# A mixture-of-experts decoder block in split float32: low and high rows side by side in the twelve full groups of experts

## The chip, the cores and the metric

The kernel runs on one NeuronCore of one Trainium2 chip. The time of a run is the device time in microseconds (us) of that core. The kernel before took 3754.32 us as the median of three runs (3741.82 to 3757.93). Beside these runs stands one profiled execution, from which every duration below is read.

## The reference, cut to what matters

The reference is a two-part decoder: a first block (attention, a linear recurrence, and a layer of 16384 experts), then a second block (a state-space mixer and sparse attention). The change concerns the layer of experts alone. Each of 256 tokens picks 128 experts out of 16384, 16 for each of 8 heads:

```python
    def expert_block(args):
        hx, ex, wx = args
        ug = jnp.take(u, ex, axis=0)
        act = jax.nn.gelu(jnp.einsum('thkd,td->thk', ug, hx)) * wx
        vg = jnp.take(vt, ex, axis=0)
        return jnp.einsum('thk,thkd->td', act, vg)
```

## The kernel before, in words

**All experts, densely.** The kernel does not gather experts. It multiplies all tokens with all 128 tiles of 128 experts (`peer_u`, 2048 inputs each), takes the gelu, multiplies with a dense matrix of weights that is zero where a token did not pick an expert, and multiplies the result with `peer_v`. Tiles 0 to 31 are treated earlier, under other work. Tiles 32 to 127 are the **full groups**: 12 passes of one loop, each with 8 tiles of `peer_u` (chunks 0 to 7) and then the 8 chunks of `peer_v` that belong to them (chunks 8 to 15).

**Split numbers.** In this stage a float32 number is written as high + low, both of the type float32r. A product of w and F is then three matmuls: w_hi times F_hi, w_hi times F_lo, w_lo times F_hi. The rows F (2048 inputs by 256 tokens, as 16 blocks of 128 by 256) are split once into `Fhi` and `Flo`. The weights are split as they arrive: a chunk lands by DMA in one of the four slots of `ring`, ScalarE (ACT) copies half a chunk (8 blocks of 128 by 128) to `vhi` (`v_high`, L1182), and VectorE (DVE) subtracts, `vlo` = chunk - `vhi` (`v_low`, L1732). `vhi` and `vlo` have two halves each, so a half is filled again only when TensorE (PE) has used it: `v_used` counts the halves that PE has finished, `vhi_ready` and `vlo_ready` the halves that are filled.

**A tile of experts on PE** (`gemm_experts`, L498): per half a wait for `vhi_ready`, 16 matmuls of 256 columns with `vhi` (against `Fhi` and `Flo` in turn, L509 and L510), a wait for `vlo_ready`, 8 matmuls of 256 columns with `vlo` (L514). All 48 add up in the first 256 columns of one PSUM bank. Banks are used in turn (tile n in bank n mod 4).

**A chunk of `peer_v` on PE** (`gemm_rows`, L540): per half 8 matmuls of 512 columns with `vhi` (L557, L558) and 4 with `vlo` (L564). They need the hidden values of the group as `Ghi` and `Glo`, and `g_ready` counts the tiles for which both stand.

**What ACT and DVE do beside it.** In the loop over the 8 tiles, ACT has for tile n: `half_high(n+1, 0)`, `half_high(n+1, 1)`, `gelu(n)` (from the bank into `GL`, L1222, then a drain), `gelu_high(n-1)` (`GL` to `Ghi`, L1227). DVE has: `half_low(n+1, 0)`, `vector` (half of a product with a vector for a modulation that is needed later, L1809), `half_low(n+1, 1)`, `weigh(n)` (`GL` times the dense weights, L1792), `gelu_low(n-1)` (`GL` - `Ghi` into `Glo`, L1797, then a drain). In both lists an instruction that waits holds up everything behind it on its engine: each engine takes its instructions in the written order. There is no planner; the order is that of the code. `GL` has two places, tile n in place n mod 2, and `gelu_free` keeps ACT from filling a place again too early.

**The DMA queue** is SP's (L450 to L457): it loads chunk c + 4 into a slot when PE has freed it, and after every second chunk the next megabyte for `vector`, once DVE has freed that buffer (`vec_free`).

Of the kernel before, what the change touches and what calls it, by code (L numbers as in the profile page):

```python
# [19 lines left out]
F32 = mybir.dt.float32  # L20
F32R = mybir.dt.float32r
# [3 lines left out]
ALU = mybir.AluOpType  # L25
ACT = mybir.ActivationFunctionType
AX = mybir.AxisListType.X

P = 128
T = 256  # L30
D = 2048
KT = D // P
# [79 lines left out]
def build(nc, a):  # L112

    ctx = ExitStack()
    with ctx:
        def sb(name, shape, dt=F32):
            return ctx.enter_context(nc.sbuf_tensor(name, shape, dt))
# [4 lines left out]

        ring = sb("ring", [P, R, KT, P])
        x = sb("x", [P, KT, T])
        rows = ExitStack()
        with rows:
            H = rows.enter_context(nc.sbuf_tensor("H", [P, KT, T], F32))
        Flo = sb("Flo", [P, KT, T], F32R)
        scale_row = H[0:1, 0:8, :].rearrange("p a (b c) -> p (a b) c", b=2)
        beside = ExitStack()  # L130
        with beside:
            head_vec = beside.enter_context(nc.sbuf_tensor("head_vec", [P, 3, D], F32))
# [36 lines left out]
        var = sb("var", [P, 2, T])  # L169
        sd = sb("sd", [P, 2, T])  # L170
        rstd = sb("rstd", [P, 2, T])
        NA = 18800
        BELOW = 2 * T + 2 * (8 * T + 4 * 512)
        shared = ExitStack()
        with shared:
            arena = shared.enter_context(nc.sbuf_tensor("arena", [P, NA], F32))
        below = sb("below", [P, BELOW])
        Ghi2 = sb("Ghi2", [P, 8, T], F32R)
        Glo2 = sb("Glo2", [P, 8, T], F32R)
        Fhi = sb("Fhi", [P, KT, T], F32R)  # L180
        above = sb("above", [P, NA - BELOW - 32 * T])
        banks = [ctx.enter_context(nc.psum_tensor(f"bank{i}", [P, 512], F32)) for i in range(4)]
        WA = ctx.enter_context(nc.psum_tensor("work_a", [P, 512], F32))
# [27 lines left out]
        r = Region()  # L211
# [22 lines left out]
        r = Region()  # L234
# [3 lines left out]
        GL = rstd  # L238
        spread_at = r.at
        spread = r(2, P, 64)  # L240
        r = Region(spread_at)
        hid = r(2, 8, T)
        Wg = r(2, 4, 8, 64)
        vbuf = hid.rearrange("p a b c -> p a (b c)")
        assert r.at == BELOW
        G_hi, G_lo = [Ghi, Ghi2], [Glo, Glo2]
        r = Region(5 * T)
        k12 = r(2, HEADS, P)
# [14 lines left out]
        r = Region()  # L263
# [18 lines left out]
        r = Region()  # L282
# [8 lines left out]
        r = Region(ssm_at - 2 * PAIRS * 16)  # L291
# [4 lines left out]
        r = Region()  # L296
# [11 lines left out]
        r = Region(nsa_at)  # L308
# [15 lines left out]
        bank_free = [sem(f"bank{i}_free") for i in range(4)]  # L324
# [13 lines left out]
        def s(name):  # L338

            if name not in S:  # L340
                S[name] = sem(name)
            return S[name]

        for name in ("consts_ready cond_ready prod_ready biased merged_scaled "
                     "disc_e disc_saved c_col_ready scale_in_psum scale_row scale_col lam_ready cond_loaded disc_loaded w1b_used "
                     "squares_ready scaled_squares sums_ready var_ready sd_ready scaled_ready f_in_psum f_ready "
                     "log1p_ready gatew_loaded qk_ready vt_ready cm_ready scores_ready negmax_ready "
                     "exps_ready probs_ready xc_ready gates_in_psum lru_u_ready lru_t_ready lru_sq_ready "
                     "ly_ready lru_done vrows_in_psum vrows_ready pt_in_psum pt_ready attn_in_psum attn_ready "
                     "k_loaded peerq_ready s_in_psum s_ready vs_ready vs_exp picked_ready cols_in_psum hot_ready "  # L350
                     "fhi_ready flo_ready hot_used spread_copied block_copied early_gelu gelu_ready weighed ghi_ready g_ready vhi_ready vlo_ready v_used y_done y_turned y_clear sz_made hhi_ready h_ready whi_ready wlo_ready half_done ssm_loaded disc_a disc_b disc_c disc_done "
                     "masks_built u_ready bu_in_psum bu_read frac_ready table_ready z_ready q_ready "
                     "y_pair gelu_free glu_free y_read y_gelu sig_ready w1_loaded kv_ready vr_in_psum vr_ready "
                     "b1e_ready cmp_gelu cmp2_in_psum kc_ready vc_in_psum gt_in_psum vg_ready q_ready2 "
                     "sn_in_psum negmax2 exps2 probs2 ptn_in_psum ptn_ready on_in_psum sz_ready combined "
                     "out_ready stored").split():
            s(name)
# [3 lines left out]
        def meet(eng, state):  # L361
# [7 lines left out]
                       dve=('lru_done', 's_ready', 'g_ready', 'combined'))  # L369
# [111 lines left out]
        def _(pe):  # L481
            mm = nc.tensor.matmul
# [14 lines left out]

            def gemm_experts(i, n, before):  # L498

                out = banks[n % 4][:, 0:T]  # L500
                pe.wait_ge(bank_free[n % 4], uses[n % 4] + before + n // 4 + 1)
                for half in range(2):
                    q = 64 + 32 * i + 2 * n + half
                    u_hi, u_lo = [w[:, half].rearrange("p k n -> p (k n)").rearrange("p (k n) -> p k n", k=8)
                                  for w in (vhi, vlo)]
                    pe.wait_ge(s("vhi_ready"), q + 1)
                    for k in range(8):
                        kk = 8 * half + k
                        mm(out, u_hi[:, k, :], Fhi[:, kk, :], start=(kk == 0), stop=False)  # L509
                        mm(out, u_hi[:, k, :], Flo[:, kk, :], start=False, stop=False)  # L510
                    pe.wait_ge(s("vlo_ready"), q + 1)
                    for k in range(8):
                        kk = 8 * half + k
                        last = mm(out, u_lo[:, k, :], Fhi[:, kk, :], start=False, stop=(kk == KT - 1))  # L514
                        if half == 1 and k == 0:
                            last.then_inc(slot_free[n % R], 1)
                    last.then_inc(s("v_used"), 1)

            def gemm_split(stage, i, pos, c, out, bank, need=None, halves=(0, 1), rows=None):

# [91 lines left out]
            for kt in range(KT):  # L612
                i, pos = kt // 2, 2 * (kt % 2) + 1
# [82 lines left out]
            with pe.Fori(0, 2) as i:  # L696
                for h in range(4):
                    n = 4 * i + h
# [267 lines left out]
        def _(act):  # L966
# [248 lines left out]
            with act.Fori(0, 12) as i:  # L1215
                act.dma_start(Wg[:, 0].rearrange("p a b c -> p a (b c)"), a["dense"][i + 4]).then_inc(prep_loaded[0], 16)

                def gelu(n):
                    act.wait_ge(s("v_used"), 64 + 32 * i + 2 * n + 2 + 2)

                    act.wait_ge(s("gelu_free"), 8 * i + n + 1)
                    A(GL[:, n % 2, :], banks[n % 4][:, 0:T], ACT.Gelu_apprx_tanh).then_inc(bank_free[n % 4], 1)  # L1222
                    act.drain().then_inc(s("gelu_ready"), 1)

                def gelu_high(n):
                    act.wait_ge(s("weighed"), 32 + 8 * i + n + 1)
                    A(Ghi[:, n, :], GL[:, n % 2, :], ACT.Copy).then_inc(s("ghi_ready"), 1)  # L1227

                def half_high(c, half):
                    v_high("peer", i, 64 + 32 * i + 2 * c, half, c)  # L1230

                for half in range(2):
                    half_high(0, half)
                for n in range(8):
                    for half in range(2):
                        half_high(n + 1, half)
                    gelu(n)
                    if n > 0:
                        gelu_high(n - 1)
                gelu_high(7)  # L1240
                for c in range(9, 16):
                    for half in range(2):
                        half_high(c, half)
# [181 lines left out]
        def _(dve):  # L1425
# [358 lines left out]
            with dve.Fori(0, 12) as i:  # L1784

                def weigh(n):

                    b = GL[:, n % 2, :].rearrange("p (a b) -> p a b", a=4)
                    if n == 0:
                        dve.wait_ge(prep_loaded[0], 64 + 16 * (i + 1))  # L1790
                    dve.wait_ge(s("gelu_ready"), 8 * i + n + 1)
                    v.tensor_tensor(b, b, Wg[:, 0, :, n, :], ALU.mult).then_inc(s("weighed"), 1)  # L1792

                def gelu_low(n):

                    dve.wait_ge(s("ghi_ready"), 32 + 8 * i + n + 1)
                    v.tensor_tensor(Glo[:, n, :], GL[:, n % 2, :], Ghi[:, n, :].bitcast(F32), ALU.subtract)\  # L1797
                        .then_inc(s("g_ready"), 1)
                    dve.drain().then_inc(s("gelu_free"), 1)

                def half_low(c, half):
                    v_low(64 + 32 * i + 2 * c, half, c)

# [13 lines left out]
                for n in range(8):  # L1817
                    half_low(n + 1, 0)
                    vector(n // 2, n % 2)
                    half_low(n + 1, 1)  # L1820
                    weigh(n)
                    if n > 0:
                        gelu_low(n - 1)
                gelu_low(7)
                for c in range(9, 16):
                    half_low(c, 0)
# [445 lines left out]
```

## Time and profile before

| | |
|---|---|
| median of three runs | 3754.32 us (3741.82 to 3757.93) |
| the profiled execution's own time | 3746.21 us |
| its span | 3744.5 us |
| mean granted TensorE clock | 0.968 |
| busy: PE, DVE, ACT, POOL | 95%, 64%, 36%, 10% of the span |
| the twelve full groups | about 1234 to 2301 us, 88.8 us each |

The span is the time from the first to the last instruction in the trace. The clock is the share of full speed that was granted to TensorE, which has two levels, 1.2 and 2.4 GHz. "Busy" counts the time in which at least one instruction of an engine was under way. Matmuls overlap in the trace (one of 256 columns is shown as 282 ns, but the next starts some 118 ns after it), so their pace is read from start to start. The same holds, to a smaller degree, for ACT and DVE: the next instruction often starts some 0.09 us before the shown end of the one before.

### The profile page before, as it was taken

How to read it: one execution, taken by the hardware profiler on the slowest of the kernel's cores; microseconds unless marked ns; L12 is line 12 of the kernel's file. 1: busy time of each engine (PE TensorE's matmuls, PEld its weight loads, DVE VectorE, ACT ScalarE, POOL GpSimd, SP SyncE). 2: the span in 40 equal slices, each digit the busy share in tenths (PEclk: the TensorE clock that was granted, in tenths of full speed). 3: DMA queues.
4: the chain of work that ended last, by engine and by line, in shares of the span. 5: the costliest groups of instructions: out<-in, count | busy, mean ns of one | idle time of the engine just before them, and what ended most of it. 6: DMA issues, size and time to landing. Idle time of an engine off the chain costs nothing. (4 is left out here: it accounts for less than half of the span.)

```text
span 3744.5 us, 57483 instructions
## 1 busy us (share of the span) xinstructions
PE 3569.6 (95%) x21190; PEld 3133.8 (84%) x21190; DVE 2386.0 (64%) x4257; ACT 1337.4 (36%) x1996; POOL 385.5 (10%) x402
## 2 busy tenths in 40 slices
PE   6899898989989999999999998999999899999998
PEld 1688787878977999999999997666689899999998
DVE  3456534887457777777777777888726541655664
ACT  0333202212234444444444444221213442555553
POOL 0000021420000000000000000677700000000000
PEclk8999999999999999999999999999999996999999
DMA  8677644654765878888888875222246550455543
GB/s 358 237 301 286 258 158 165 225 192 155 268 252 205 298 289 300 295 302 297 291 298 287 300 292 192 79 90 90 101 169 254 212 180 24 180 181 186 189 170 131
DMA packets 123313, 817.72 MB, mean 218 GB/s; under 512 B 12848, under 2 KB 18224, under 8 KB 27184
## 3 DMA queue, kind: packets, MB, share of 16 engines
q1 hardware_dynamic: 105552, 760.26, 55.6%
q10 hardware_dynamic: 17632, 55.63, 3.8%
q8 instruction: 93, 1.52, 0.2%
q14 instruction: 36, 0.29, 0.0%
HBM read 791.66 MB, written 24.18 MB: 218 GB/s over the span
## 5 line engine op out<-in xcount | busy, mean ns | idle before, releaser
L494 PE MATMUL bank<-H,ring 128*128 128x256 f32 x4352 | 980.4, 385 | 45.8 <-ACT H L1013 17.5
L494 PEld LDWEIGHTS bank<-H,ring 128*128 128x128 f32 x4352 | 829.4, 193 | 183.8 <-issue 72.1
L1732 DVE TENSOR_TENSOR vlo<-ring,vhi 128x1024 fp32r<-128x1024 f32 x448 | 548.2, 1225 | 307.1 <-ACT vhi L1182 294.0
L1182 ACT ACTIVATE vhi<-ring 128x1024 fp32r<-128x1024 f32 x448 | 474.9, 1060 | 626.7 <-PE bank L564 350.6
L1448 DVE TENSOR_TENSOR wlo<-ring,whi 128x1024 fp32r<-128x1024 f32 x240 | 293.9, 1225 | 324.4 <-ACT whi L984 318.3
L530 PE MATMUL bank<-Hhi,whi 128*128 128x256 f32 x1920 | 481.7, 288 | 17.3 <-DVE Hlo L1459 10.2
L531 PE MATMUL bank<-Hlo,whi 128*128 128x256 f32 x1920 | 474.9, 285 | 0.0
L557 PE MATMUL bank<-vhi,Ghi 128*128 128x512 f32 x1024 | 400.8, 391 | 0.0
L558 PE MATMUL bank<-vhi,Glo 128*128 128x512 f32 x1024 | 400.5, 391 | 0.0
L530 PEld LDWEIGHTS bank<-Hhi,whi 128*128 128x128 f32 x1920 | 369.6, 192 | 23.2 <-issue 16.9
L509 PE MATMUL bank<-Fhi,vhi 128*128 128x256 f32 x1536 | 371.3, 282 | 0.0
L531 PEld LDWEIGHTS bank<-Hlo,whi 128*128 128x128 f32 x1920 | 370.6, 193 | 0.0
L510 PE MATMUL bank<-Flo,vhi 128*128 128x256 f32 x1536 | 370.5, 280 | 0.0
L984 ACT ACTIVATE whi<-ring 128x1024 fp32r<-128x1024 f32 x240 | 253.9, 1059 | 307.3 <-PE bank L535 288.6
L510 PEld LDWEIGHTS bank<-Flo,vhi 128*128 128x128 f32 x1536 | 289.2, 188 | 0.5
L509 PEld LDWEIGHTS bank<-Fhi,vhi 128*128 128x128 f32 x1536 | 289.1, 188 | 0.5
L564 PE MATMUL bank<-vlo,Ghi 128*128 128x512 f32 x1024 | 276.4, 392 | 12.5 <-DVE vlo L1732 12.5
L535 PE MATMUL bank<-Hhi,wlo 128*128 128x256 f32 x1920 | 270.9, 284 | 0.0
L535 PEld LDWEIGHTS bank<-Hhi,wlo 128*128 128x128 f32 x1920 | 249.0, 192 | 0.0
L564 PEld LDWEIGHTS bank<-vlo,Ghi 128*128 128x128 f32 x1024 | 192.4, 189 | 56.0 <-DVE vlo L1732 15.8
L1809 DVE CUSTOM_DVE_ANT_0 arena<-arena,cond 128x1024 f32<-128x1024 f32 x192 | 234.0, 1219 | 0.0
L557 PEld LDWEIGHTS bank<-vhi,Ghi 128*128 128x128 f32 x1024 | 192.9, 188 | 41.4 <-issue 0.6
(404 smaller groups left out, 4379.1 us busy)
## 6 DMA issues: line engine op xcount, KB each, us to landing
ring<-in_peer_u SPq DMA_DIRECT2D x128, 1024.0 KB, 5.0
ring<-in_peer_v SPq DMA_DIRECT2D x128, 1024.0 KB, 5.0
arena<-in_w_mod SPq DMA_DIRECT2D x96, 1024.0 KB, 6.7
ring<-in_w_qz SPq DMA_DIRECT2D x64, 1024.0 KB, 4.8
ring<-in_w_ada SPq DMA_DIRECT2D x56, 1024.0 KB, 5.8
ring<-in_w_in SPq DMA_DIRECT2D x40, 1024.0 KB, 6.1
ring<-in_w_mod SPq DMA_DIRECT2D x32, 1024.0 KB, 5.7
ring<-in_ssm_in SPq DMA_DIRECT2D x32, 1024.0 KB, 5.1
```

What stands on the lines that cost most here:

```text
L494: last = mm(out, ring[:, pos % R, k, :], rhs[:, k, :], start=(k == 0), stop=(k == KT - 1))
L509: mm(out, u_hi[:, k, :], Fhi[:, kk, :], start=(kk == 0), stop=False)
L510: mm(out, u_hi[:, k, :], Flo[:, kk, :], start=False, stop=False)
L530: mm(out, whi[:, half, k, :], Hhi[:, kk, :], start=(kk == 0), stop=False)
L531: mm(out, whi[:, half, k, :], Hlo[:, kk, :], start=False, stop=False)
L535: last = mm(out, wlo[:, half, k, :], Hhi[:, kk, :], start=False, stop=(kk == KT - 1))
L557: mm(pair[th][:], G_hi[part][:, n, tok], vhi[:, half, k, :], start=(n == 0), stop=False)
L558: mm(pair[th][:], G_lo[part][:, n, tok], vhi[:, half, k, :], start=False, stop=False)
L564: last = mm(pair[th][:], G_hi[part][:, n, tok], vlo[:, half, k, :], start=False, stop=(n == 7))
L1182: A(vhi[:, half], v_half(pos, half), ACT.Copy).then_inc(s("vhi_ready"), 1)
L1448: v.tensor_tensor(wlo[:, half], ring[:, pos % R, 8 * half:8 * half + 8, :], whi[:, half].bitcast(F32), ALU.subtract).then_inc(s("wlo_ready ...
L1732: v.tensor_tensor(vlo[:, half], v_half(pos, half), vhi[:, half].bitcast(F32), ALU.subtract)\
```

## The change

The rows get one tensor, `FF`, with the low rows first and the high rows behind them, so that both can be read as the 512 columns of one matmul. `Flo` and `Fhi` are now its two halves. For that, H and the arena are placed elsewhere in SBUF, which adds or removes no instruction.

On PE a half of a tile now is: 7 matmuls of `vhi` with both rows (512 columns, the whole bank), the wait for `vlo_ready`, 8 matmuls of `vlo` with the high rows into the second half of the bank, and the eighth matmul of `vhi`. The bank then holds high-times-low in its first 256 columns and the other two products in its last 256, and the two have to be added on the way out: ACT copies the first half to `GL` (`Copy`, new), DVE adds the second half to it in place (`hidden_sum`, new), ACT takes the gelu of `GL` in place. The order of both lists changes too: `gelu_high(n-1)` and `gelu_low(n-1)` now stand ahead of the second half of chunk n+1.

```diff
@@ gemm_experts, on PE
-                out = banks[n % 4][:, 0:T]
+                bank = banks[n % 4]
...
+                    def by_high(k):
+                        kk = 8 * half + k
+                        return mm(bank[:].rearrange("p (a b) -> p a b", a=2), u_hi[:, k, :], FF[:, :, kk, :],
+                                  start=(kk == 0), stop=(kk == KT - 1))
+
                     pe.wait_ge(s("vhi_ready"), q + 1)
-                    for k in range(8):
-                        kk = 8 * half + k
-                        mm(out, u_hi[:, k, :], Fhi[:, kk, :], start=(kk == 0), stop=False)
-                        mm(out, u_hi[:, k, :], Flo[:, kk, :], start=False, stop=False)
+                    for k in range(7):
+                        by_high(k)
                     pe.wait_ge(s("vlo_ready"), q + 1)
                     for k in range(8):
-                        kk = 8 * half + k
-                        last = mm(out, u_lo[:, k, :], Fhi[:, kk, :], start=False, stop=(kk == KT - 1))
+                        last = mm(bank[:, T:2 * T], u_lo[:, k, :], Fhi[:, 8 * half + k, :], start=False, stop=False)
                         if half == 1 and k == 0:
                             last.then_inc(slot_free[n % R], 1)
-                    last.then_inc(s("v_used"), 1)
+                    by_high(7).then_inc(s("v_used"), 1)
@@ the loop over the groups, on ACT
                     act.wait_ge(s("gelu_free"), 8 * i + n + 1)
-                    A(GL[:, n % 2, :], banks[n % 4][:, 0:T], ACT.Gelu_apprx_tanh).then_inc(bank_free[n % 4], 1)
+                    A(GL[:, n % 2, :], banks[n % 4][:, 0:T], ACT.Copy).then_inc(s("low_copied"), 1)
+                    act.wait_ge(s("hidden_summed"), 8 * i + n + 1)
+                    A(GL[:, n % 2, :], GL[:, n % 2, :], ACT.Gelu_apprx_tanh)
                     act.drain().then_inc(s("gelu_ready"), 1)
...
                 for n in range(8):
-                    for half in range(2):
-                        half_high(n + 1, half)
-                    gelu(n)
+                    half_high(n + 1, 0)
                     if n > 0:
                         gelu_high(n - 1)
+                    half_high(n + 1, 1)
+                    gelu(n)
                 gelu_high(7)
@@ the loop over the groups, on DVE
+                def hidden_sum(n):
+
+                    dve.wait_ge(s("low_copied"), 8 * i + n + 1)
+                    v.tensor_tensor(GL[:, n % 2, :], banks[n % 4][:, T:2 * T], GL[:, n % 2, :], ALU.add)\
+                        .then_inc(bank_free[n % 4], 1)
+                    dve.drain().then_inc(s("hidden_summed"), 1)
...
                 for n in range(8):
                     half_low(n + 1, 0)
                     vector(n // 2, n % 2)
-                    half_low(n + 1, 1)
-                    weigh(n)
                     if n > 0:
                         gelu_low(n - 1)
+                    half_low(n + 1, 1)
+                    hidden_sum(n)
+                    weigh(n)
                 gelu_low(7)
```

On ACT, in the loop over the groups, one tile of experts before (the second copy of a chunk, the gelu, the high part of the tile ahead of it, the next chunk's first copy; the names in brackets are the counters that the instruction waits for):

```order
L1182 ACTIVATE vhi<-ring 128x1024 [waits v_used]
L1221 REGISTER_ALU [waits v_used]
L1222 ACTIVATE rstd<-bank 128x256 [waits gelu_free]
L1226 REGISTER_ALU
L1227 ACTIVATE Ghi<-rstd 128x256 [waits weighed]
L1181 REGISTER_ALU [waits slot3_loaded]
L1182 ACTIVATE vhi<-ring 128x1024 [waits v_used]
```

The same place now:

```order
L1186 ACTIVATE vhi<-ring 128x1024 [waits v_used]
L1225 REGISTER_ALU [waits v_used]
L1226 ACTIVATE rstd<-bank 128x256 [waits gelu_free]
L1228 ACTIVATE rstd<-rstd 128x256 [waits hidden_summed]
L1185 REGISTER_ALU [waits slot3_loaded]
L1186 ACTIVATE vhi<-ring 128x1024 [waits v_used]
L1232 REGISTER_ALU
L1233 ACTIVATE Ghi<-rstd 128x256 [waits weighed]
```

`rstd` is the tensor in which `GL` lives. The gelu (now L1228) waits for DVE, and the copy of the next chunk to `vhi` stands directly behind it.

On DVE, in the same loop, one tile before, from the second `v_low` of a chunk on:

```order
L1732 TENSOR_TENSOR vlo<-ring,vhi 128x1024 [waits vhi_ready]
L1791 REGISTER_ALU
L1792 TENSOR_TENSOR rstd<-rstd,arena 128x256 [waits gelu_ready]
L1796 REGISTER_ALU
L1797 TENSOR_TENSOR Glo<-rstd,Ghi 128x256 [waits ghi_ready]
L1731 REGISTER_ALU
L1732 TENSOR_TENSOR vlo<-ring,vhi 128x1024 [waits vhi_ready]
L1809 ISA arena,sd<-arena,cond 128x1024 [waits vec1_loaded]
L1809 ISA sd 128x1
```

The same place now:

```order
L1738 TENSOR_TENSOR vlo<-ring,vhi 128x1024 [waits vhi_ready]
L1809 REGISTER_ALU
L1810 TENSOR_TENSOR rstd<-bank,rstd 128x256 [waits low_copied]
L1798 TENSOR_TENSOR rstd<-rstd,arena 128x256 [waits gelu_ready]
L1737 REGISTER_ALU
L1738 TENSOR_TENSOR vlo<-ring,vhi 128x1024 [waits vhi_ready]
L1822 ISA arena,sd<-arena,cond 128x1024 [waits vec1_loaded]
L1822 ISA sd 128x1
L1802 REGISTER_ALU
L1803 TENSOR_TENSOR Glo<-rstd,Ghi 128x256 [waits ghi_ready]
```

The sum of the halves (now L1810) stands behind the second `v_low` of the next chunk, and `gelu_low` has moved from ahead of the next first `v_low` to behind `vector`.

## Rows read from the trace of the kernel before

**Rows 1.** The page: the span, and section 1.

```profile
span 3744.5 us, 57483 instructions
PE 3569.6 (95%) x21190; PEld 3133.8 (84%) x21190; DVE 2386.0 (64%) x4257; ACT 1337.4 (36%) x1996; POOL 385.5 (10%) x402
```

**Rows 2.** Windows of 89 us, one per group; then the sum of twelve.

```profile
core 0: us, PE busy (x) PEld busy (x) DVE busy (x) ACT busy (x) POOL busy (x), PEclk, DMA share, GB/s
1590.00:1679.00 89.00, 89.00 (x579) 81.47 (x578) 68.06 (x90) 39.37 (x48) 0.00 (x0) 1.00 0.82 298
...
sum 1068.00, PE 1067.91 PEld 977.46 DVE 815.14 ACT 471.28 POOL 0.00; mean PE 88.99 PEld 81.45 DVE 67.93 ACT 39.27 POOL 0.00
```

**Rows 3.** Waits, 1234 to 2300 us: who waited for whom, total, times, longest.

```profile
ACT vhi L1182 <- PE bank L514: 274.5, 192, 1.8
DVE vlo L1732 <- ACT vhi L1182: 246.9, 372, 1.6
```

**Rows 4.** Timeline of PE, a half of a tile: start, duration, instruction.

```profile
1602.17 0.28 PE L509 MATMUL bank<-Fhi,vhi 128*128 128x256 f32 x1
...
1605.01 0.28 PE L509 MATMUL bank<-Fhi,vhi 128*128 128x256 f32 x1
```

**Rows 5.** Timeline of PE, half a chunk of `peer_v`, 12 matmuls.

```profile
1641.56 0.39 PE L557 MATMUL bank<-vhi,Ghi 128*128 128x512 f32 x1
...
1644.28 0.39 PE L557 MATMUL bank<-vhi,Ghi 128*128 128x512 f32 x1
```

**Rows 6.** Timeline of ACT, the same stage; in brackets idle time before it.

```profile
1602.36 1.06 ACT L1182 ACTIVATE vhi<-ring 128x1024 fp32r<-128x1024 f32 x1 [1.78 <-PE bank L514]
1603.33 0.36 ACT L1222 ACTIVATE rstd<-bank 128x256 f32<-128x256 f32 x1
1603.87 0.42 ACT L1227 ACTIVATE Ghi<-rstd 128x256 fp32r<-128x256 f32 x1 [0.18 <-issue]
1605.21 1.06 ACT L1182 ACTIVATE vhi<-ring 128x1024 fp32r<-128x1024 f32 x1 [0.92 <-PE bank L514]
...
1636.30 1.06 ACT L1182 ACTIVATE vhi<-ring 128x1024 fp32r<-128x1024 f32 x1 [1.76 <-PE bank L514]
```

**Rows 7.** Timeline of DVE, the same stage.

```profile
1603.46 1.23 DVE L1732 TENSOR_TENSOR vlo<-ring,vhi 128x1024 fp32r<-128x1024 f32 x1 [0.47 <-ACT vhi L1182]
1604.60 0.42 DVE L1792 TENSOR_TENSOR rstd<-rstd,arena 128x256 f32<-128x256 f32 x1
1604.93 0.42 DVE L1797 TENSOR_TENSOR Glo<-rstd,Ghi 128x256 fp32r<-128x256 f32 x1
...
1607.45 1.22 DVE L1809 CUSTOM_DVE_ANT_0 arena<-arena,cond 128x1024 f32<-128x1024 f32 x1
1608.59 0.08 DVE L1809 DVE_READ_ACCUMULATOR2_ANT sd<- 128x1 f32 x1
```

**Rows 8.** Single lines: durations in ns (least/median/most) of like operations, other stages.

```profile
L2007 DVE TENSOR_TENSOR arena<-work_a,H x16: 424/425/426, 3210.9 to 3624.1; 128x256 f32<-128x256 f32 x16
L1296 ACT ACTIVATE arena<-arena x4: 1039/1039/1056, 2710.5 to 2713.4; 128x1024 f32<-128x1024 f32 x4
L1062 ACT ACTIVATE arena<-arena x8: 507/508/509, 158.2 to 433.9; 128x256 f32<-128x256 f32 x8
L509 PEld LDWEIGHTS bank<-Fhi,vhi x1536: 186/188/193, 1235.1 to 2256.9; 128*128 128x128 f32 x192
```

**Rows 9.** Timeline, the state-space stage: DVE drains, ACT and DVE follow.

```profile
2443.55 0.69 DVE L1868 SCALAR_TENSOR_TENSOR sd<-work_d,sd 128x512 f32<-128x512 f32 x1
...
2444.39 0.63 ACT L1262 ACTIVATE y<-sd 128x512 f32<-128x512 f32 x1 [2.82 <-DVEq L1869]
...
2444.44 0.70 DVE L1887 TENSOR_TENSOR work_d<-work_b,y 128x512 f32<-128x512 f32 x1 [0.20 <-issue]
```

**Rows 10.** Windows elsewhere, columns as in rows 2.

```profile
2351.00:2700.00 349.00, 345.53 (x1445) 240.61 (x1446) 291.33 (x537) 68.94 (x121) 265.91 (x308) 0.99 0.24 90
3082.00:3153.00 71.00, 68.41 (x369) 67.25 (x369) 11.73 (x30) 14.70 (x28) 0.00 (x0) 0.59 0.04 16
```

More of the change, by code:

```diff
@@ L124, in build @@
         x = sb("x", [P, KT, T])
[L125 to L129, printed above, removed]
         beside = ExitStack()
@@ L171, in build @@
         rstd = sb("rstd", [P, 2, T])
+        rows = ExitStack()
+        with rows:
+            H = rows.enter_context(nc.sbuf_tensor("H", [P, KT, T], F32))
+        scale_row = H[0:1, 0:8, :].rearrange("p a (b c) -> p (a b) c", b=2)
         NA = 18800
@@ L175, in build @@
         with shared:
+            shared.enter_context(nc.sbuf_tensor("under_arena", [P, KT, T], F32))
             arena = shared.enter_context(nc.sbuf_tensor("arena", [P, NA], F32))
+        FF = sb("FF", [P, 2, KT, T], F32R)
+        Flo, Fhi = FF[:, 0], FF[:, 1]
         below = sb("below", [P, BELOW])
@@ L179, in build @@
         Glo2 = sb("Glo2", [P, 8, T], F32R)
-        Fhi = sb("Fhi", [P, KT, T], F32R)
         above = sb("above", [P, NA - BELOW - 32 * T])
@@ L240, in build @@
         spread = r(2, P, 64)
-        r = Region(spread_at)
+        r = Region(16 * T + spread_at)
         hid = r(2, 8, T)
@@ L244, in build @@
         vbuf = hid.rearrange("p a b c -> p a (b c)")
-        assert r.at == BELOW
+        assert r.at == 16 * T + BELOW
         G_hi, G_lo = [Ghi, Ghi2], [Glo, Glo2]
@@ L350, in build @@
                      "k_loaded peerq_ready s_in_psum s_ready vs_ready vs_exp picked_ready cols_in_psum hot_ready "
-                     "fhi_ready flo_ready hot_used spread_copied block_copied early_gelu gelu_ready weighed ghi_ready g_ready vhi_ready vlo_ready v_used y_done y_turned y_clear sz_made hhi_ready h_ready whi_ready wlo_ready half_done ssm_loaded disc_a disc_b disc_c disc_done "
+                     "fhi_ready flo_ready hot_used spread_copied hidden_summed block_copied early_gelu gelu_ready low_copied weighed ghi_ready g_ready vhi_ready vlo_ready v_used y_done y_turned y_clear sz_made hhi_ready h_ready whi_ready wlo_ready half_done ssm_loaded disc_a disc_b disc_c disc_done "
                      "masks_built u_ready bu_in_psum bu_read frac_ready table_ready z_ready q_ready "
```

## The prediction

> **What bounds the kernel now.** I read the page first: PE is busy for 95% of the span, DVE for 64%, ACT for 36% [rows 1]. That is a mean over stages, so I looked at the changed stage alone. In windows of 89 us, one per group, PE is busy for the whole of each, the clock stands at its upper level (1.00), DVE is busy for 68 of 89 us and ACT for 39 [rows 2]. The waits of the stage say the same from the other side: ACT waits for PE (192 times, 1.8 us at most), DVE waits for ACT, and PE itself is never idle [rows 2, 3]. So PE sets the pace here, and DVE has 21 us of room per group, ACT 50. With that reading alone a change that saves PE time and adds 0.8 us of short instructions per tile is a small gain. The question is whether the room of ACT and DVE lies where the new work falls, so I wrote down their order.
>
> The pace before: six tiles of ACT's copies take 1636.30 - 1602.36 = 33.94 us, so a tile (48 matmuls) takes 5.66 us, 0.118 us per matmul of 256 columns [rows 6]; PE's own rows give 2.84 us for one half [rows 4]. A half chunk of `peer_v` takes 2.72 us for 12 matmuls, 0.227 us per matmul of 512 columns [rows 5]. A group is 8 x 5.66 + 16 x 2.72 = 88.8 us, and twelve are 1066 us, as the windows show.
>
> **PE's part of the change.** Per tile 32 matmuls of 256 columns become 16 of 512, and 16 of 256 remain: 16 x 0.227 + 16 x 0.118 = 5.51 us, 0.15 us less than 5.66. If PE stays the bound, that is 0.15 x 96 tiles = 14 us. The number of columns is the same, so nothing more can be had.
>
> The Trainium skill ("TensorE: Matmul & The Clock Gate", section on the back-to-back issue gap) states an isolated gap of N/2.4 + 2.5 ns at the upper clock: 109 ns for 256 columns, 216 ns for 512, so that merging two saves 2.5 ns. The trace's paces are 118 and 227 ns, and merging two saves 9 ns. By the page the 14 us would be 4 us; my sum below needs neither.
>
> **ACT's and DVE's part.** Before, the two engines only follow PE: ACT's gelu needs nothing from DVE. Now tile n goes ACT copy, DVE sum, ACT gelu, and because each engine takes its instructions in order, a closed chain appears from one tile to the next:
>
> sum(n) on DVE, gelu(n) on ACT, first copy of chunk n+2 to `vhi` on ACT (queued behind the gelu), its `vlo` on DVE, `vector`, `gelu_low(n)`, second `vlo` of chunk n+2, sum(n+1).
>
> None of these waits for PE once the chain is late, and every tile goes through it once. Its length, link by link:
> - two `vlo`: from the start of one to the next instruction 1604.60 - 1603.46 = 1.14 us, so 2.28 [rows 7];
> - the sum: a like instruction that reads a bank and SBUF, 256 columns, takes 0.42 [rows 8];
> - from a drained DVE instruction to ACT: 2444.39 - (2443.55 + 0.69) = 0.15 [rows 9];
> - the gelu from SBUF: a copy of that size from SBUF takes 0.42 (gelu_high), and the gelu of 1024 columns from SBUF takes 1.04, no more than the 1.06 of a copy of 1024; so 0.42; then 0.18 for the drain before ACT's next instruction [rows 6, 8];
> - the copy to `vhi` 1.06, and 0.04 until DVE starts (1602.36 + 1.06 to 1603.46) [rows 6, 7];
> - `vector`, with the read of its sum: 1608.59 + 0.08 - 1607.45 = 1.22 [rows 7];
> - `gelu_low` 0.42, and 0.20 for its drain (2444.24 to 2444.44), which before lay in DVE's idle time ahead of `v_low` [rows 7, 9].
>
> Sum: 2.28 + 0.42 + 0.15 + 0.60 + 1.10 + 1.22 + 0.62 = 6.39 us, against PE's 5.51. So this chain becomes the bound of the tile part, and PE waits about 0.9 us per tile for the first half of `vhi`. The copy out of the bank, `weigh`, `gelu_high` and the second copy to `vhi` run beside it on the other engine and cost nothing; PE's 14 us are not seen either.
>
> **One group after.** Start of PE's first tile to sum(0): 5.51 (the tile) + 0.20 (PE to ACT, 1605.01 to 1605.21) + 1.10 + 1.14 = 7.95 us [rows 4, 6]. Then seven rounds of the chain, 7 x 6.39 = 44.73. From sum(7) to PE's first matmul with chunk 9, the second of `peer_v` (the first one's halves stand already, and PE runs out of them): sum 0.42, hop 0.15, gelu 0.42, drain and hop 0.15, `weigh` 0.42, hop 0.04, `gelu_high` 0.42, copy 1.06, hop and weight load 0.24 (0.19 of it [rows 8]), together 3.32. Then 14 halves of 2.72 = 38.08, in which PE bounds again: there ACT has one copy per half, DVE at most 1.14 + 1.22. Together 94.1 us against 88.8: 5.3 more per group, 12 x 5.3 = 64 us (+1.7%).
>
> **Other queues.** SP issues its loads by the slots that PE frees and by `vec_free`, which the second half of `vector` signals; `vector` keeps its place behind the first `v_low`. The bytes per group are unchanged at a DMA share of 0.82 [rows 2], and a group of 94 us lowers that, so I price DMA at nothing. The bank is freed some 4 us later (by the sum, not the gelu), but it is needed again only three tiles on: nothing. The other placement in SBUF: nothing, as it moves no instruction.
>
> **Bounds of the unknown links.** The trace has no such chain, so its hops are from elsewhere. Low end: all hops 0.04, drains free, gelu 0.36 as from the bank, `gelu_low` at its 0.33 issue distance (1604.60 to 1604.93): 2.28 + 0.42 + 0.04 + 0.36 + 1.10 + 1.22 + 0.33 = 5.75 us, still above 5.51; the group is then 7.95 + 40.25 + 2.76 + 38.08 = 89.0 us, +3 us in all. High end: no overlap of `vlo` (2.46), hops and drains 0.20, gelu 0.51 (an activation of another kind, 256 columns [rows 8]), `vector` 1.30: 7.0 us, a group of 99 us, +123 us. I take 6.39, since each link stands on the row nearest to it.
>
> **Rivals.**
> - *The chain is hidden* (the other side). If a round took under 5.51 us, PE would stay the bound, and the kernel would gain 14 us: 3746 - 14 = 3732 us in the terms of the profiled execution, not slower. For it: 21 us of idle DVE per group. Against it: the bare instructions of a round, without a hop or a drain, are 2.28 + 0.42 + 0.42 + 1.06 + 1.22 + 0.33 = 5.73 us, and they stand one behind the other by their waits and their order. It decides at 0.88 us less per round. Chance 0.05.
> - *The chain binds, but barely* (its low end, 5.75 to 5.9 us): +3 to +18 us, 3749 to 3764 us. Chance 0.05.
> - *The clock falls.* PE now pauses 0.9 us in every 6.4. For it: in one stage with PE busy for 68 of 71 us the mean clock was 0.59. Against it: in the state-space stage, where PE idles for 3.5 of 349 us, it was 0.99, and in the groups themselves 1.00 [rows 2, 10]. A fall first eats the pauses: PE's step is 5.51/clock and passes the chain only under 0.86. At 0.75 it is 7.35 us, another 0.96 x 96 = 92 us, about 3902 us. Chance 0.04.
> - *The chain is longer than I think* (7 us, the high end): up to 3870 us. Chance 0.06.
>
> The Trainium skill (same page, section "A second HAM failure mode: psum-queue depth-cycling") says that a kernel whose TensorE pauses shortly between groups of matmuls had its clock go up and down. It speaks for the clock rival; no stretch of this trace pauses as often as the tiles will, so no row here tests it.
>
> **How the numbers follow.** My forecast, a round of 6.1 to 6.8 us, has chance 0.80. Its time is 3746.2 (the profiled execution) + 64 = 3810 us; that execution lies 8 us under the median of the three runs, which spread over 16 us, so I set 3812. A round of 6.1 us gives +39 us and one of 6.8 us +98 us by the same group, so 3785 to 3844; I widen that to 3780 to 3850, which leaves out the hidden chain, the bare one, the clock and most of the long chain. A difference under 0.5% (19 us) can't be told from no change here. Slower by more: the forecast, the clock and the long chain, 0.90. Within 0.5%: the bare chain and most of the hidden chain (14 us is 0.4%), 0.08. Faster: 0.02.
>
> **What would show it.** In the profile after: PE idle ahead of the matmuls on `FF` about 0.9 us per tile, put down to ACT's `vhi`, some 80 times, and a longer gap ahead of the second chunk of `peer_v`; ACT's gelu waiting for DVE about once per tile (the copy done early, the sum late); the distance of two sums on DVE near 6.4 us; groups of 94 us; paces of 0.227 and 0.118 us within a half, clock 1.00. I am wrong if the sums lie 5.5 us apart and PE is busy for the whole of a window; my links are wrong in size if the distance is another than 6.4; the rival of the clock shows as matmul paces twice as long.

## The result, and the profile after

| | before | after |
|---|---|---|
| median of the runs | 3748.28 us (3741.82 to 3757.93, 4 runs) | 3808.45 us (3808.09 to 3810.16, 4 runs) |
| profiled execution, span | 3746.21, 3744.5 us | 3808.09, 3806.4 us |
| twelve groups, first tile to the turn of the result | 1068.0 us = 12 x 89.00 | 1119.5 us = 12 x 93.29 |
| state-space stage behind them | 407.2 us | 420.2 us |

The changed kernel takes 1.0153 times as long, 95% interval 1.0124 to 1.0182 (the two medians alone give 1.016). 3812 us and "slower" were forecast. The state-space stage is counted from the first product that turns the groups' result to the first gelu of its own output. The span grew by 61.9 us: 51.5 in the groups, 13.0 in the state-space stage, -2.7 before the groups (they begin at 1232.6 us instead of 1235.3), and 0.1 in the rest. The -2.7 is spread and not the change: over the twelve profiles of this document the groups begin anywhere from 1230.6 to 1241.4 us. The first of these is the forecast one, though smaller than 64; the second was not foreseen.

The page's head after, which answers to [rows 1]:

```profile
span 3806.4 us, 54711 instructions
PE 3584.6 (94%) x19654; PEld 3061.2 (80%) x19654; DVE 2441.6 (64%) x4353; ACT 1359.7 (36%) x2092; POOL 385.5 (10%) x402
```

PE issues 1536 matmuls fewer, and its share fell by one point only. DVE's share, 64%, is that of before. Nothing here tells of a new bound.

One group in a window, the columns as in [rows 2]:

```profile
1600.00:1694.00 94.00, 90.98 (x453) 75.89 (x452) 72.11 (x98) 41.83 (x57) 0.00 (x0) 1.00 0.78 281
```

PE was busy for the whole of a window; now it is idle for 3.0 us in 94. The clock is still 1.00, and the DMA share went from 0.82 to 0.78. The waits of the groups (engine, what it writes, whom it waited for: us in total, times, longest), beside [rows 3]:

```profile
ACT rstd L1228 <- DVEq L1812: 260.6, 96, 3.1
...
PEld bank L510 <- ACT vhi L1186: 32.2, 49, 0.8
PE bank L561 <- ACT vhi L1186: 19.9, 24, 1.2
...
PE bank L510 <- ACT vhi L1186: 16.5, 48, 0.4
```

The first row is new and the largest: ACT's gelu stands 96 times, once for each of the 96 tiles, for the drained sum on DVE. Ahead of the gelu ACT's own work ends early, and behind it the copies to `vhi` come late, so that PE waits for them.

Here is one round of the chain, on DVE from one sum to the next (start, duration, instruction, idle time before it):

```profile
1644.93 0.42 DVE L1810 TENSOR_TENSOR rstd<-bank,rstd 128x256 f32<-128x256 f32 x1
...
1645.90 0.43 DVE L1798 TENSOR_TENSOR rstd<-rstd,arena 128x256 f32<-128x256 f32 x1 [0.55 <-ACTq L1229]
...
1647.11 1.23 DVE L1738 TENSOR_TENSOR vlo<-ring,vhi 128x1024 fp32r<-128x1024 f32 x1 [0.78 <-ACT vhi L1186]
1648.25 1.22 DVE L1822 CUSTOM_DVE_ANT_0 arena<-arena,cond 128x1024 f32<-128x1024 f32 x1
1649.39 0.09 DVE L1822 DVE_READ_ACCUMULATOR2_ANT sd<- 128x1 f32 x1
1649.39 0.42 DVE L1803 TENSOR_TENSOR Glo<-rstd,Ghi 128x256 fp32r<-128x256 f32 x1
1650.03 1.23 DVE L1738 TENSOR_TENSOR vlo<-ring,vhi 128x1024 fp32r<-128x1024 f32 x1 [0.21 <-issue]
1651.17 0.42 DVE L1810 TENSOR_TENSOR rstd<-bank,rstd 128x256 f32<-128x256 f32 x1
```

The first and the last sum of the same group, and PE's first products of it, from which the mean round and the group are read further on:

```profile
1605.47 1.79 PE L510 MATMUL bank<-FF,vhi 128*128 128x512 f32 x7
1613.51 0.42 DVE L1810 TENSOR_TENSOR rstd<-bank,rstd 128x256 f32<-128x256 f32 x1
1657.48 0.42 DVE L1810 TENSOR_TENSOR rstd<-bank,rstd 128x256 f32<-128x256 f32 x1
```

And on ACT:

```profile
1645.42 0.42 ACT L1228 ACTIVATE rstd<-rstd 128x256 f32<-128x256 f32 x1 [3.07 <-DVEq L1812]
1646.02 1.06 ACT L1186 ACTIVATE vhi<-ring 128x1024 fp32r<-128x1024 f32 x1 [0.17 <-issue]
1646.98 0.40 ACT L1233 ACTIVATE Ghi<-rstd 128x256 fp32r<-128x256 f32 x1
1647.29 1.04 ACT L1186 ACTIVATE vhi<-ring 128x1024 fp32r<-128x1024 f32 x1
1648.23 0.36 ACT L1226 ACTIVATE rstd<-bank 128x256 f32<-128x256 f32 x1
...
1651.67 0.42 ACT L1228 ACTIVATE rstd<-rstd 128x256 f32<-128x256 f32 x1 [3.08 <-DVEq L1812]
```

Read the two in turn. The sum at 1644.93 lets the gelu start at 1645.42; behind its drain the copy starts at 1646.02; DVE has stood 0.78 us for that copy and starts `vlo` at 1647.11; then DVE runs without a gap but for the drain, up to the next sum at 1651.17. The round is 6.24 us. ACT meanwhile stands 3.08 us for DVE. Both engines are idle in every round, and neither could start sooner in this order: each waits for a link on the other.

On PE (a row with x7 is seven instructions):

```profile
1646.36 0.40 PE L510 MATMUL bank<-FF,vhi 128*128 128x512 f32 x1
1647.13 1.90 PE L510 MATMUL bank<-FF,vhi 128*128 128x512 f32 x7 [0.37 <-ACT vhi L1186]
1648.87 1.12 PE L518 MATMUL bank<-FF,vlo 128*128 128x256 f32 x8
1649.82 2.03 PE L510 MATMUL bank<-FF,vhi 128*128 128x512 f32 x8
...
1660.41 0.49 PE L561 MATMUL bank<-vhi,Ghi 128*128 128x512 f32 x1 [1.17 <-ACT vhi L1186]
```

The 0.77 us between the starts of the first two rows would be 0.23 in a stream: PE loses 0.54 us at the first half of each tile. The page shows only 0.37 of it as idle, because the shown end of a matmul lies behind its turn in the stream. The last row is the longer gap ahead of chunk 9.

### The profile page after: what moved, and what is told of

Same layout as the page of the kernel before. It is cut to its first block and busy times, and to the rows that moved or that the text cites. A ratio compares the mean times of both kernels' runs of the same rounds, so it can differ in the third digit from the quotient of the medians.

```text
span 3806.4 us, 54711 instructions
## 1 busy us (share of the span) xinstructions
PE 3584.6 (94%) x19654; PEld 3061.2 (80%) x19654; DVE 2441.6 (64%) x4353; ACT 1359.7 (36%) x2092; POOL 385.5 (10%) x402
## 5 line engine op out<-in xcount | busy, mean ns | idle before, releaser
L510 PE MATMUL bank<-FF,vhi 128*128 128x512 f32 x1536 | 403.7, 398 | 16.5 <-ACT vhi L1186 16.5
L510 PEld LDWEIGHTS bank<-FF,vhi 128*128 128x128 f32 x1536 | 276.1, 188 | 81.4 <-ACT vhi L1186 32.2
L562 PEld LDWEIGHTS bank<-vhi,Glo 128*128 128x128 f32 x1024 | 193.1, 189 | 39.7
L518 PEld LDWEIGHTS bank<-FF,vlo 128*128 128x128 f32 x1536 | 208.8, 188 | 17.4
```

The source lines that it names most:

```text
L510: return mm(bank[:].rearrange("p (a b) -> p a b", a=2), u_hi[:, k, :], FF[:, :, kk, :], start=(kk == 0), stop=(kk == KT - 1))
L562: mm(pair[th][:], G_lo[part][:, n, tok], vhi[:, half, k, :], start=False, stop=False)
```

## The experiments

"Groups" is the length of the twelve groups in the profiled execution, read as in the table above. Two theories stood against each other: the closed chain between ACT and DVE sets the round, or PE itself became slower by the wide products, the new order or the new placement.

**Two parts of the change alone.** The first kernel is the one before with the new placement: `Flo` and `Fhi` lie side by side, the arena and `H` elsewhere.

```diff
-        Flo = sb("Flo", [P, KT, T], F32R)
...
+        FF = sb("FF", [P, 2, KT, T], F32R)
+        Flo, Fhi = FF[:, 0], FF[:, 1]
...
-        Fhi = sb("Fhi", [P, KT, T], F32R)
```

> The kernel before, with nothing but the changed kernel's placement in SBUF (low and high rows in one tensor, H and the arena elsewhere). Theory (a closed chain ACT-DVE in the groups costs 52 us, and the 13 us that the state-space stage lost come from the placement): groups stay at 88.8 us, the state-space stage grows by 13 us, time 13 us over before. Rival (the state-space stage fell into another rhythm between DVE and GpSimd, which timing and not placement decides): groups 88.8 us, time as before, or 13 us more in some executions and not in others.

It took 3752.89 us beside 3754.68 for the kernel before, ratio 1.0005 (0.9993 to 1.0017). But its groups grew from 1068.0 to 1076.8 us, 0.73 us each. It is PE's pace. The copies of ACT follow PE one for each half of a tile:

```profile
1605.75 1.06 ACT L1183 ACTIVATE vhi<-ring 128x1024 fp32r<-128x1024 f32 x1 [1.82 <-PE bank L515]
1608.63 1.06 ACT L1183 ACTIVATE vhi<-ring 128x1024 fp32r<-128x1024 f32 x1 [0.95 <-PE bank L515]
1611.51 1.06 ACT L1183 ACTIVATE vhi<-ring 128x1024 fp32r<-128x1024 f32 x1 [1.82 <-PE bank L515]
```

Half a tile takes 2.88 us, where it was 2.85 and 2.84 in [rows 6] and [rows 4]; a matmul of 256 columns 0.120 us instead of 0.118. So the placement costs 8.8 us in the profile as long as PE is the bound; both expectations had the groups unchanged and missed that. The state-space stage took 408.2 us, so the placement doesn't lengthen it. The ratio doesn't show it, most likely because the runs of the kernel before lie in two bunches, near 3742 and near 3757 us, and those of this one, 3751.33 to 3756.88, about 10 us above the lower one (more on that in the next section).

The second has the new order of both lists, and nothing else.

```diff
-                    for half in range(2):
-                        half_high(n + 1, half)
-                    gelu(n)
+                    half_high(n + 1, 0)
                     if n > 0:
                         gelu_high(n - 1)
+                    half_high(n + 1, 1)
+                    gelu(n)
...
-                    half_low(n + 1, 1)
-                    weigh(n)
                     if n > 0:
                         gelu_low(n - 1)
+                    half_low(n + 1, 1)
+                    weigh(n)
```

> The kernel before, with nothing but the new order of both lists (gelu_high and gelu_low of tile n-1 ahead of the second half of chunk n+1); no sum, no 512-column product. Theory: without the sum there is no closed chain, DVE and ACT have room, PE stays never idle, groups of 88.8 us, no change within 5 us. Rival (the new order itself delays the second half of vlo, behind gelu_low and its drain): PE waits at vlo_ready, groups of 90 us or more, over 15 us slower.

Groups 1068.1 us, 89.01 each; 3756.32 us, ratio 1.0006 (0.999 to 1.0022). The order alone costs the groups nothing. This profile has a state-space stage of 420.8 us, as long as after the change (its own time is 3757.35 us).

```profile
1590.00:1679.00 89.00, 89.00 (x579) 81.50 (x579) 68.08 (x90) 38.55 (x48) 0.00 (x0) 1.00 0.81 297
```

**The wide product undone.** The changed kernel, with two products of 256 columns in place of one of 512:

```diff
-                        return mm(bank[:].rearrange("p (a b) -> p a b", a=2), u_hi[:, k, :], FF[:, :, kk, :],
-                                  start=(kk == 0), stop=(kk == KT - 1))
+                        mm(bank[:, 0:T], u_hi[:, k, :], Flo[:, kk, :], start=(kk == 0), stop=False)
+                        return mm(bank[:, T:2 * T], u_hi[:, k, :], Fhi[:, kk, :], start=False, stop=(kk == KT - 1))
```

> The changed kernel with each 512-column product made as two of 256 again (low rows into the first half of the bank, high rows into the second); sum and order as changed. PE's own work per tile is 5.66 us instead of 5.51. Theory (the chain of 6.25 us per tile sets the pace): the same time as the changed kernel, 3808 us within 3. Rival (PE's work still counts in full, the chain adds to it): 0.15 x 96 = 14 us more, 3822 us.

Groups 1121.4 us, 93.45 each, 0.16 more than after: PE's form of product hardly matters here, since PE isn't the bound.

```profile
1600.00:1693.00 93.00, 90.56 (x577) 81.82 (x576) 71.27 (x97) 40.96 (x57) 0.00 (x0) 1.00 0.78 283
```

With 577 matmuls in place of 453 in the window, PE is still idle for 2.4 us of 93: the longer products went into its pauses. The total was 3800.42 us, 1.0129 (1.0109 to 1.0148), which is less than after, though the groups are longer: this profile has the short state-space stage, 407.6 us. The 3808 us expected counted on the long one.

**The chain opened.** The sum and its wait go, and the gelu reads the upper half of the bank. The product of high weights and low rows is left out of the result; PE's work is that of the changed kernel.

```diff
-                    A(GL[:, n % 2, :], banks[n % 4][:, 0:T], ACT.Copy).then_inc(s("low_copied"), 1)
-                    act.wait_ge(s("hidden_summed"), 8 * i + n + 1)
-                    A(GL[:, n % 2, :], GL[:, n % 2, :], ACT.Gelu_apprx_tanh)
+                    A(GL[:, n % 2, :], banks[n % 4][:, T:2 * T], ACT.Gelu_apprx_tanh).then_inc(bank_free[n % 4], 1)
...
-                    hidden_sum(n)
```

> The changed kernel without the sum of the two halves: ACT takes the gelu straight from the second half of the bank, so the product of high weights and low rows is left out of the result; no copy, no hidden_sum. Theory: the chain is open, PE bounds the groups again with its 5.51 us per tile: groups of 87.6 us instead of 93.15, 12 x 5.5 = 66 us less than the changed kernel, 3742 us (3729 if the state-space stage is back at its shorter time as well). Rival (the wide product reading two places of SBUF, or the order, costs the time): groups stay near 93 us, 3800 us or more.

Groups 1063.5 us, 88.62 each, where 87.6 was expected; 3740.06 us, 0.9972 (0.9959 to 0.9984). PE never idles again, and the theory that PE became slower falls:

```profile
1594.00:1683.00 89.00, 89.00 (x452) 75.69 (x451) 68.15 (x90) 39.09 (x50) 0.00 (x0) 1.00 0.83 297
```

It also gives the price of PE's own part, undisturbed:

```profile
1601.19 2.03 PE L510 MATMUL bank<-FF,vhi 128*128 128x512 f32 x8
1603.06 1.12 PE L518 MATMUL bank<-FF,vlo 128*128 128x256 f32 x8
1604.01 2.02 PE L510 MATMUL bank<-FF,vhi 128*128 128x512 f32 x8
```

Eight wide products take 1603.06 - 1601.19 = 1.87 us, 0.234 each, not the 0.227 of `peer_v` in [rows 5]. PE's own part of the change saves 1068.0 - 1063.5 = 4.5 us, not 14. Against the first experiment, which has the same placement and the narrow products, it is 1076.8 - 1063.5 = 13.3 us: merging gives about what was forecast, and the placement takes 8.8 of it back (the order costs nothing by the second experiment). Not all of the 13.3 is the wide product's. By the mean distance of two starts over the groups, two narrow ones took 0.2398 us and the wide one 0.2329, which is 7 ns, 11 us in all; the low products beside them took 0.1185 us instead of 0.1199, which is another 2 us.

**The same work inside and beside the chain.** Both kernels add one DVE instruction of 256 columns and a drain per tile to the changed kernel (its output is what it was), once ahead of the sum, once behind `weigh`.

```diff
+                def extra():
+
+                    v.tensor_tensor(var[:, 1], var[:, 1], var[:, 1], ALU.max)
+                    dve.drain()
...
+                    extra()
                     hidden_sum(n)
                     weigh(n)
```

> The changed kernel with one more instruction on DVE per tile, a maximum of an unused scratch of 256 columns with itself, and a drain (0.42 us and 0.2 us), ahead of hidden_sum, in the closed chain. Theory: every round grows by about 0.6 us, 8 x 0.6 x 12 = 58 us more than the changed kernel, about 3866 us. Rival (PE waits for something else, or DVE's room of over 20 us per group takes it up): no change, 3808 us.

Groups 1173.5 us, 97.79 each, 4.5 more than after; 3853.09 us, 1.0274 (1.023 to 1.0317). The round went from 6.28 to 6.83 us:

```profile
1644.21 0.42 DVE L1816 TENSOR_TENSOR var<-var 128x256 f32<-128x256 f32 x1
1644.78 0.42 DVE L1810 TENSOR_TENSOR rstd<-bank,rstd 128x256 f32<-128x256 f32 x1 [0.15 <-issue]
...
1651.03 0.42 DVE L1816 TENSOR_TENSOR var<-var 128x256 f32<-128x256 f32 x1
1651.61 0.42 DVE L1810 TENSOR_TENSOR rstd<-bank,rstd 128x256 f32<-128x256 f32 x1 [0.15 <-issue]
```

The added 0.57 us is the instruction and its drain, as seen between these rows. The time grew by less than the groups, 45 us, because this profile has the short state-space stage, 407.4 us; so has the next one, 408.1 us. Behind `weigh` the same edit:

> The same extra instruction and drain, but behind weigh, where DVE idles some 0.8 us while ACT copies the next chunk: beside the chain. Theory: no change against the changed kernel within 5 us (3808 us, or 13 us less with the shorter rhythm of the state-space stage). Rival (DVE's total work is the bound): as much more as with the instruction in the chain, about 58 us.

Groups 1117.9 us, 93.16 each, as after; 3797.34 us, 1.0121 (1.0082 to 1.016). The instruction falls into DVE's wait for ACT:

```profile
1647.17 0.42 DVE L1810 TENSOR_TENSOR rstd<-bank,rstd 128x256 f32<-128x256 f32 x1
1648.48 0.42 DVE L1816 TENSOR_TENSOR var<-var 128x256 f32<-128x256 f32 x1
1649.35 1.23 DVE L1738 TENSOR_TENSOR vlo<-ring,vhi 128x1024 fp32r<-128x1024 f32 x1 [0.45 <-ACT vhi L1186]
...
1653.42 0.42 DVE L1810 TENSOR_TENSOR rstd<-bank,rstd 128x256 f32<-128x256 f32 x1
```

DVE's wait ahead of `vlo` shrank from 0.78 to 0.45 us, and the round is 6.25. The same busy time on the same engine costs 54 us of groups (1173.5 - 1119.5) in one place and nothing in the other. This pair shows the chain most plainly, and DVE's total work falls as a cause.

**Shortening the chain.** The calculation of the chosen experts' rows, `vector`, need not lie between the two `vlo` of a chunk. Behind the sum it is out of the chain:

```diff
                     half_low(n + 1, 0)
-                    vector(n // 2, n % 2)
                     if n > 0:
                         gelu_low(n - 1)
                     half_low(n + 1, 1)
                     hidden_sum(n)
+                    vector(n // 2, n % 2)
                     weigh(n)
```

> The changed kernel with vector moved on DVE from behind the first v_low of a chunk to behind hidden_sum, where DVE waits for the gelu anyway. Same instructions, same results. Theory (closed chain of 6.25 us per tile): vector's 1.15 us leaves the chain, 5.10 us is under PE's step, so the tiles run at PE's pace (5.64 us per tile as in the run without the sum); only after tile 7 PE still waits about 0.9 us for chunk 9, since weigh(7) is now behind vector. Groups of 89.5 us, 45 us less than the changed kernel: about 3751 us, 3764 with the longer rhythm of the state-space stage. Rival (DVE's total work is the bound, not the order): nothing gained, 3800 us.

Groups 1073.0 us, 89.42 each; 3753.21 us, 1.0001 (0.9985 to 1.0017). The tiles run at PE's pace again, and the gap ahead of chunk 9 is what is left:

```profile
1642.65 0.49 PE L561 MATMUL bank<-vhi,Ghi 128*128 128x512 f32 x1 [0.50 <-ACT vhi L1186]
```

So the next kernel also lets `gelu_high(7)` follow the first copy of chunk 9 instead of preceding it:

```diff
-                gelu_high(7)
                 for c in range(9, 16):
                     for half in range(2):
                         half_high(c, half)
+                        if c == 9 and half == 0:
+                            gelu_high(7)
```

> As the run before, and on ACT gelu_high(7) behind the first copy of chunk 9, so that PE does not wait for that copy at the end of the tiles. Theory: PE never idle in the groups, 88.6 us each as without the sum, 3740 us (3753 with the longer rhythm of the state-space stage), 0.3% under the kernel before. Rival (the wait at chunk 9 has another cause): as the run before, 89.5 us a group.

Groups 1063.6 us, 88.63 each, the same as with the chain opened; 3743.29 us, 0.9972 (0.9954 to 0.9989) of the kernel before. PE is busy for the whole of a window:

```profile
1595.00:1684.00 89.00, 89.00 (x452) 75.67 (x451) 71.65 (x99) 43.08 (x57) 0.00 (x0) 1.00 0.81 297
```

This is the fastest version that keeps the whole computation, 0.28% under the kernel before, with an interval that leaves 1 out. Only part of this edge is the groups' 4.4 us: all its runs, 3738.55 to 3747.37, lie where the lower bunch of the kernel before does, and that one has the upper bunch as well.

**Both kernels once more,** for the state-space stage.

> The kernel before, unchanged, profiled once more. In the runs so far its times lie in two bunches, about 3741 and 3757 us. Theory (the state-space stage, whose code and data none of the experiments touches, settles in one of two rhythms between DVE and GpSimd, 407 or 420 us long): this profile shows groups of 89.0 us and a stage of either 407 or 420 us, and its own time goes with it. Rival (the length of that stage belongs to the kernel, by its placement or its code): 407 us again, and the two bunches come from elsewhere.

> The changed kernel, unchanged, profiled once more. Theory: groups of 93.2 us again; the state-space stage of 407 or 420 us, and the time 3795 or 3808 us with it. Rival (the longer stage belongs to this kernel): 420 us and 3808 us every time.

Before again: 3754.49 us (3744.63 to 3760.66), groups 1068.0, stage 407.2. After again: 3809.92 us (3806.51 to 3813.91), 1.015 (1.0124 to 1.0175), groups 1119.6, stage 419.5. The groups repeat to 0.1 us. The profiled execution of before again took 3752.33 us with the short stage, 6 us more than the first one, because its groups began at 1241.4 us instead of 1235.3: a time alone doesn't tell which stage it had. The stage is taken up in the next section.

## Why the prediction was right, point by point

- *A closed chain becomes the bound of the tile part.* Right, and shown from three sides: opened, it costs nothing; lengthened, it costs what was added; the same work beside it is free. With `vector` out of it PE is the bound again.
- *A round of 6.39 us.* Measured 1657.48 - 1613.51 = 43.97 us for seven, 6.28 each. Two links were sized too long. From the drained sum to ACT it is 1645.42 - (1644.93 + 0.42) = 0.07 us, where 0.15 was taken from [rows 9], an instruction of another kind and size. And `vector` costs 1649.39 - 1648.25 = 1.14, not 1.22, since `gelu_low` starts together with the read of the accumulator, which I had counted in full. The rest came as forecast: gelu with drain 1646.02 - 1645.42 = 0.60, `gelu_low` with drain 1650.03 - 1649.39 = 0.64 beside 0.62.
- *One group, 94.1 us.* Measured from PE's first tile at 1605.47 to that of the next group: 8.04 to the first sum (7.95 forecast), 43.97 (44.73), from the last sum to chunk 9 1660.41 - 1657.48 = 2.93 (3.32), and 38.2 for the other halves (38.08), together 93.15. The end was too long by the same hops. So the group was forecast 5.3 us longer and became 4.3: 51.5 us in all.
- *PE's 14 us, hidden.* Hidden, yes; its size was wrong for the change as it stands. With the chain open PE saves 4.5 us against the kernel before, not 14. Only at the same placement is it 13.3 us, of which the merging is some 11. The Trainium skill ("TensorE: Matmul & The Clock Gate", section "Back-to-back issue gap") gave 2.5 ns a merge, by which I had worked out 4 us; the merge itself measured 7 ns. That 4.5 us lies near those 4 is luck, since the placement, of which that figure says nothing, is in it.
- *The other placement: nothing.* Wrong in size. Alone it costs 8.8 us, and with the chain open it takes PE's gain from 13.3 down to 4.5. Beside the chain nothing of it is seen, since PE has 0.6 us to spare per round. "It moves no instruction" was no reason.
- *PE waits 0.9 us per tile.* About 0.6: PE's step is 2 x (1.87 + 0.95) = 5.64 us by the kernel with the open chain, not 5.51, against a round of 6.28.
- *DMA and the banks: nothing.* Right; the DMA share fell, and no wait on either came up.
- *The clock rival.* Fell: 1.00 in the windows of the groups. The Trainium skill ("TensorE: Matmul & The Clock Gate", section "A second HAM failure mode: psum-queue depth-cycling") spoke for it; pauses of 0.5 us in every 6.3 left the clock at its upper level here. *The hidden chain and the bare one:* fell with the measured round. *The longer chain:* fell on the other side; the round is shorter than forecast.
- *Nothing happens outside the groups.* This was the silent premise of the sum, and it failed by 13 us in the state-space stage. That 3812 lies so near 3808 is in part luck: this offset the 12 us that the groups were forecast too long.

**The 13 us.** In this stage DVE computes the angles (`var<-iota_t,arena`, L1865 before, L1879 after). Their durations (count: least/median/most in ns), before:

```profile
L1865 DVE TENSOR_SCALAR var<-iota_t,arena x32: 344/428/1129, 2338.6 to 2682.1; 128x256 f32<-128x256 f32 x32
```

and after:

```profile
L1879 DVE TENSOR_SCALAR var<-iota_t,arena x32: 343/967/1319, 2387.4 to 2742.8; 128x256 f32<-128x256 f32 x32
```

The same 32 instructions, with the same least time and more than twice the median; together they take 16.6 us before and 32.6 after. Here is a long one in after, with GpSimd's beside it:

```profile
2551.08 1.27 POOL L2172 TENSOR_TENSOR arena<-arena,y 128x512 f32<-128x512 f32 x1 [0.67 <-DVEq L1912]
2551.19 1.31 DVE L1879 TENSOR_SCALAR var<-iota_t,arena 128x256 f32<-128x256 f32 x1 [0.23 <-issue]
```

And the one of the same place in before:

```profile
2544.38 0.72 POOL L2162 TENSOR_TENSOR arena<-arena 128x256 f32<-128x256 f32 x1 [0.21 <-issue]
2544.69 0.57 DVE L1865 TENSOR_SCALAR var<-iota_t,arena 128x256 f32<-128x256 f32 x1 [0.23 <-issue]
```

In both GpSimd starts first, and the DVE instruction ends 0.15 us after GpSimd's (0.16 by these rounded rows): at 2552.50 behind 2551.08 + 1.27 = 2552.35, and at 2545.26 behind 2544.38 + 0.72 = 2545.10. The same holds in these two profiles whenever a GpSimd instruction is under way as the angle starts, 30 of 32 times before (once with 0.19) and 29 of 32 after. What differs is which one it is: of 256 columns and 0.72 us before, of 512 columns and 1.27 us after. The Trainium skill ("SBUF — State Buffer", section "SBUF: two separate sides") says that the two engines share a pair of ports, which a GpSimd instruction or a DVE one in a 2-port mode takes whole for its duration; these rows agree, though they don't show in which mode DVE's runs. So the stage has two rhythms, by which GpSimd instruction the angles meet. Over twelve profiles it took either 407 to 409 us (before twice, and seven of the experiments) or 419 to 421 (after twice, and the kernel with the new order alone).

What chooses the rhythm isn't shown. It went with one thing in all twelve profiles: the granted clock 50 us into the stage, when PE is busy for 9 of 12 us. That comes first: in after the angles take longer than before only from 82 us into the stage on. After, and then the kernel with the extra instruction beside the chain, whose code in this stage is the same:

```profile
2402.00:2414.00 12.00, 9.04 (x33) 6.60 (x32) 11.00 (x20) 2.26 (x4) 9.36 (x13) 0.86 0.01 2
```

```profile
2404.00:2416.00 12.00, 9.14 (x27) 5.83 (x26) 11.02 (x20) 2.26 (x4) 9.46 (x13) 0.72 0.01 1
```

At a mean of 0.72 to 0.77 there the stage was short (nine profiles), at 0.86 or 1.00 long (three). That is a correlation, and no run set the clock. What is shown: the change's code doesn't fix the rhythm, since kernels with this placement are found in the short one, and one with the old placement in the long one. All eight executions of the changed kernel took 3806 to 3814 us, and all four of the kernel with the extra instruction, equal in the groups to 1.6 us, 3795 to 3798; this fits a kernel that stays in one rhythm. The executions of the kernel before lie in two bunches near 3742 and 3757 us, which would be both rhythms; both its profiles have the short one, so that stays open. At equal rhythm the change costs the 51.5 us of the groups, 1.4%; with the whole difference it is 1.5%.

## What to carry to other kernels

An engine's idle time isn't room for new work if the work makes two in-order engines wait for each other in turn: write down the closed path from one step to the same point of the next, add its links, drains and hops included, and compare the sum with the bound's step. If it is longer, look first for what lies on that path only by its place in a list: moving `vector` and one copy won back the 56 us that the chain cost in the groups (46.5 and 9.4). And give a new placement of operands a price of its own, by a kernel that has nothing else changed.

## What the runs showed of the hardware

- Where things lie in SBUF changed the matmuls' pace with no instruction changed: 0.118 to 0.120 us at 256 columns, 8.8 us in all. At the new placement a moving operand of two pieces of 256 columns ran at 0.233 to 0.234 us, while `peer_v`, with one piece of 512, has 0.227. The wide product at the old placement can't be had, since the two halves lie apart there, and why the placement matters wasn't tried.
- A DVE instruction that started behind a GpSimd one ended 0.15 us after it and so took up to four times as long (0.34 to 1.31 us); 13 us of the kernel went with which GpSimd instruction that was.
- A drained DVE instruction of 256 columns lets ACT start 0.07 us after its shown end; the next DVE instruction starts 0.15 us after it (0.22 behind `gelu_low`); an ACT instruction with a drain is followed by the next in 0.18 us.
